# One kernel's first 75 microseconds: loads first, tables on ScalarE's queue, two low halves on VectorE, bias transfers later

## The reference

```python
hn = rms_norm(h, attn_norm[0])
qkv = hn @ w_qkv + b_qkv                       # 1024 q, 128 k, 128 v columns
q = q_columns * HEAD_DIM ** -0.5
s = einsum('bqhgd,bshd->bhgqs', q, k) + head_bias(rel_table, dist)
s = where(in_window & valid, s, NEG_INF)       # window of 128 keys
p = softmax(s, with a sink per head); o = p @ v
h = h + o @ w_o + b_o
h = h + swiglu(rms_norm(h, ffn_norm[0]), w_gu, w_down)
```

## Time and profile before

| | |
|---|---|
| three runs, us | 1986.18, 1988.04, 1989.64 |
| median, us | 1988.04 |
| profiled execution, us | 1987.46, of which the span 1985.7 |
| busy share of the span | PE 97%, PEld 81%, DVE 53%, ACT 42%, POOL 40% |
| chain that ended last | PE 66%, issue 19%, POOL 8%, DVE 5%, ACT 2% |
| weight loads | 294 of 512 KB, median 3.5 us to landing |

### The profile page before, as it was taken

The page is one execution under the profiler, slowest core; times in us unless marked ns, Lnnn a source line. Parts: engine busy times, 40 slices in busy tenths (PEclk is TensorE's granted clock), DMA queues, the critical chain, the costliest instruction groups (busy, mean ns, idle before and its releaser), DMA issues.

```text
span 1985.7 us, 29356 instructions
## 1 busy us (share of the span) xinstructions
PE 1925.1 (97%) x9732; PEld 1617.1 (81%) x9732; DVE 1047.3 (53%) x2320; ACT 831.9 (42%) x1528; POOL 800.7 (40%) x395
## 2 busy tenths in 40 slices
PE   7999999999999999999999999999999899999997
PEld 5898888888878899888888887888788788777886
DVE  5565656221354777545562445656514656565645
ACT  4564222222353777542222323322222346666622
POOL 3633544444364111135444443444544233323441
PEclk9999999999999999999999999999999999999999
DMA  7632554332233113025543322223222121212121
GB/s 238 183 101 96 201 177 162 106 104 95 85 127 121 39 52 89 33 96 201 176 163 105 106 95 90 91 96 111 96 95 95 64 85 54 74 50 77 64 86 43
DMA packets 70019, 209.50 MB, mean 106 GB/s; under 512 B 9739, under 2 KB 15115, under 8 KB 69948
## 3 DMA queue, kind: packets, MB, share of 16 engines
q1 hardware_dynamic: 57724, 174.72, 26.8%
q10 hardware_dynamic: 12224, 33.85, 5.3%
HBM read 196.90 MB, written 8.49 MB: 103 GB/s over the span
## 4 chain that ended last, share of the span: by engine, by line
PE 66%; issue 19%; POOL 8%; DVE 5%; ACT 2%; POOLq 0%; DVEq 0%; ACTq 0%
PE bank L1019 16%; PE bank L1021 15%; PE bank L1020 15%; POOL wsp L470 8%; PE bank L1372 3%; PE bank L1321 2%; PE bank L1567 2%; PE bank L1422 2%; PE bank L1352 2%; PE bank L1223 1%; PE bank L1548 1%; PE bank L1559 1%; PE bank L1427 1%; PE bank L1368 1%; PE bank L1211 1%
## 5 line engine op out<-in xcount | busy, mean ns | idle before, releaser
L470 POOL TENSOR_TENSOR wsp<-raw,wsp 128x1024 fp32r<-128x1024 f32 (+2 forms) x294 | 713.4, 2433 | 942.5 <-ACT wsp L574 942.2
L1019 PE MATMUL bank<-xs,wsp 128*128 128x512 f32 x1304 | 513.8, 394 | 5.0 <-POOL wsp L470 2.4
L574 ACT ACTIVATE wsp<-raw 128x1024 fp32r<-128x1024 f32 (+2 forms) x294 | 302.6, 1037 | 512.5 <-PE bank L1021 469.0
L1021 PE MATMUL bank<-xs,wsp 128*128 128x512 f32 x1304 | 508.8, 390 | 0.0
L1020 PE MATMUL bank<-xs,wsp 128*128 128x512 f32 x1304 | 508.4, 390 | 0.0
L1019 PEld LDWEIGHTS bank<-xs,wsp 128*128 128x128 f32 x1304 | 245.6, 188 | 58.1 <-issue 8.4
L1021 PEld LDWEIGHTS bank<-xs,wsp 128*128 128x128 f32 x1304 | 245.3, 188 | 51.9
L1020 PEld LDWEIGHTS bank<-xs,wsp 128*128 128x128 f32 x1304 | 245.7, 188 | 50.1 <-issue 1.0
L1019 PE MATMUL bank<-gsp,wsp 128*128 128x512 f32 x512 | 200.1, 391 | 2.1 <-issue 1.2
L1021 PE MATMUL bank<-gsp,wsp 128*128 128x512 f32 x512 | 199.3, 389 | 0.0
L1020 PE MATMUL bank<-gsp,wsp 128*128 128x512 f32 x512 | 199.2, 389 | 0.0
(11 more groups left out here) (319 smaller groups left out, 2746.5 us busy)
## 6 DMA issues: line engine op xcount, KB each, us to landing
raw<-weights SPq DMA_DIRECT2D x294, 512.0 KB, 3.5
gen<-ada ACTq DMA_DIRECT2D x48, 512.0 KB, 3.6
tmp<-mid SPq DMA_DIRECT2D x64, 128.0 KB, 3.0
bias_b<-bias_row ACTq DMA_DIRECT2D x1, 4096.0 KB, 37.9
mid<-bias_b SPq DMA_DIRECT2D x8, 512.0 KB, 4.0
hT<-xT SPq DMA_DIRECT2D x2, 1024.0 KB, 9.5
bias_a<-bias_row ACTq DMA_DIRECT2D x1, 2048.0 KB, 17.7
mid<-bias_a SPq DMA_DIRECT2D x8, 256.0 KB, 3.0
```

The costliest lines, as they stand in the source:

```text
L470: pool.tensor_tensor(wsp[:, slot, 1, 0:w], raw[:, slot, 0:w], wsp[:, slot, 0, 0:w].bitcast(F32), ALU.subtract).then_inc(w_ready, 1)
L574: act.activation(wsp[:, u % RING, 0, 0:w], raw[:, u % RING, 0:w], ACT.Copy).then_inc(hi_done, 1)
L1019: pe.matmul(dst, w[0], x[0], start=first, stop=False)
L1021: return pe.matmul(dst, w[1], x[0], start=False, stop=last)
```

## The change

The order of the first 75 us is rewritten. Nothing behind the query units changes.

- SyncE begins with unit 0. `rel` and `onehot` move to ScalarE's queue, ahead of `colp` and `rowp`, behind the wait for the first memset.
- ScalarE runs a tiny Copy (one column) before it waits for data; the instruction stream places a table load ahead of the first activation.
- VectorE makes the low halves of units 0 and 1: unit 0 before the input's low halves, unit 1 behind them. GpSimd begins with unit 2, once `w_ready` is 2.
- ScalarE's order becomes: split unit 0, scale 4 tiles, split unit 1, scale 4 tiles, split unit 2, squares, split unit 3, copy and store the bias product, root, split unit 4, copy k, split units 5 and 6, issue `bias_a` and `bias_b`, split units 7 to 12.
- The bias product goes to banks 3 to 6 instead of 1 to 4. TensorE waits for its copies before the first query unit, not before `A_V`.
- TensorE runs filling matmuls of 128 x 128 into bank 7, which nobody reads: 9 at the start, and 2 behind each of the four bias matmuls.

```diff
 @block.sync
-            sp.wait_ge(consts, 1)
-            sp.dma_start(gen[0:32, 0:HEADS], rel).then_inc(rel_in, 16)
-            sp.dma_start(gen[0:33, 16:16 + BIAS_COLS], onehot).then_inc(rel_in, 16)
 @block.gpsimd
-            split_units(0, A_O + AHEAD)
+            pool.wait_ge(w_ready, 2)
+            for u in range(2, RING):
+                split_lo(u, u)
+            split_units(RING, A_O + AHEAD)
 @block.scalar
+            act.wait_ge(consts, 1)
+            act.dma_start(gen[0:32, 0:HEADS], rel).then_inc(rel_in, 16)
+            act.dma_start(gen[0:33, 16:16 + BIAS_COLS], onehot).then_inc(rel_in, 16)
             act.dma_start(colp[:, :], cols).then_inc(cols_in, 16)
             act.dma_start(rowp[:, :], rows.partition_broadcast(P)).then_inc(rows_in, 16)
+            act.wait_ge(consts, 4)
+            act.activation(credit[:, 11:12], eps[:, 0:1], ACT.Copy)
...
+            def bias_rows():
+                act.wait_ge(brow_mm, 4)
+                for n in range(4):
+                    w = BIAS_COLS // 4
+                    act.activation(brow[:, w * n:w * n + w], bank[3 + n][0:HEADS, 0:w], ACT.Copy).then_inc(brow_copied, 1)
+                act.wait_ge(brow_copied, 4)
+                act.dma_start(bias_row, brow).then_inc(bias_stored, 16)
             split_hi(0)
-            scaled_hi("attn0", 0)
-            for u in range(1, AHEAD):
-                split_hi(u)
...
+            scaled_hi("attn0", 0, range(4))
+            split_hi(1)
+            scaled_hi("attn0", 0, range(4, DC))
+            split_hi(2)
+            squares(0, (A_K + AHEAD,), bias_rows)
             split_hi(A_V + AHEAD)
             act.wait_ge(k_raw, 1)
             act.activation(a_ks[0:HD], a_k, ACT.Copy).then_inc(k_hi, 1)
-            with act.Fori(0, 2) as i:
-                for k in range(RING):
-                    split_hi(A_Q + k + AHEAD, i)
+            for u in range(A_Q + AHEAD, A_Q + DC + AHEAD):
+                split_hi(u)
+                if u == A_Q + AHEAD + 1:
+                    act.wait_ge(bias_stored, 16)
+                    act.dma_start(bias_a, ...).then_inc(bias_stored, 16)
+                    act.dma_start(bias_b, ...).then_inc(bias_stored, 16)
 @block.tensor
+            def keep_running(dst, count):
+                for _ in range(count):
+                    pe.matmul(dst[:, 0:P], mean_w[:, :], ident[:, :], start=True, stop=True)
+            pe.wait_ge(consts, 6)
+            keep_running(bank[7], 9)
             pe.wait_ge(rel_in, 32)
             for n in range(4):
                 w = BIAS_COLS // 4
-                pe.matmul(bank[1 + n][0:HEADS, 0:w], ...)
+                pe.matmul(bank[3 + n][0:HEADS, 0:w], ...)
+                keep_running(bank[7], 2)
-            pe.wait_ge(consts, 6)
             project(A_K, bank[0][:, :], norm=0)
-            pe.wait_ge(brow_copied, 4)
             project(A_V, bank[1][:, :])
             mean_square(0)
             for i in range(2):
                 if i:
                     ...
+                else:
+                    pe.wait_ge(brow_copied, 4)
 @block.vector
+            def split_lo(u):
+                dve.wait_ge(hi_done, u + 1)
+                if u:
+                    dve.wait_ge(w_ready, u)
+                dve.tensor_tensor(wsp[:, u % RING, 1, :], raw[:, u % RING, :], wsp[:, u % RING, 0, :].bitcast(F32),
+                                  ALU.subtract).then_inc(w_ready, 1)
+            split_lo(0)
             dve.wait_ge(cols_in, 16)
             scaled_lo(0, "attn0")
+            split_lo(1)
```

More of the change, by code:

```diff
@@ L574, in split_hi, with scaled_hi @@
                 act.activation(wsp[:, u % RING, 0, 0:w], raw[:, u % RING, 0:w], ACT.Copy).then_inc(hi_done, 1)
-            def scaled_hi(gain, base):
-                for j in range(DC):
+            def scaled_hi(gain, base, tiles=range(DC)):
+                for j in tiles:
                     if base:
@@ L583, in scaled_hi, with squares @@
                     act.activation(xs[:, 0, j, :], hT[:, j, :], ACT.Copy, scale=col(gain, j)).then_inc(xs_hi, 1)
-            def squares(n, held=()):
+            def squares(n, held=(), between=None):
                 if n >= NORM_FINAL:
@@ L600, in squares @@
                     split_hi(u)
+                if between is not None:
+                    between()
                 act.wait_ge(sq_used, 8 * n + 8)
@@ L663, in ffn @@
                 out_inputs(u0 + 2 * FC, FC, MID_FFN[n], n == 1)
+            act.wait_ge(consts, 1)
+            act.dma_start(gen[0:32, 0:HEADS], rel).then_inc(rel_in, 16)
+            act.dma_start(gen[0:33, 16:16 + BIAS_COLS], onehot).then_inc(rel_in, 16)
             act.dma_start(colp[:, :], cols).then_inc(cols_in, 16)
             act.dma_start(rowp[:, :], rows.partition_broadcast(P)).then_inc(rows_in, 16)
+            act.wait_ge(consts, 4)
+            act.activation(credit[:, 11:12], eps[:, 0:1], ACT.Copy)
             act.wait_ge(cols_in, 16)
             act.wait_ge(consts, 6)
-            split_hi(0)
-            scaled_hi("attn0", 0)
-            for u in range(1, AHEAD):
-                split_hi(u)
[L675 to L688, removed]
+            def bias_rows():
[5 more added lines that the diff above has]
+                act.dma_start(bias_row, brow).then_inc(bias_stored, 16)
+            brow = gen[0:HEADS, 2048:2048 + BIAS_COLS]
+            split_hi(0)
+            scaled_hi("attn0", 0, range(4))
[3 more added lines that the diff above has]
+            squares(0, (A_K + AHEAD,), bias_rows)
             split_hi(A_V + AHEAD)
@@ L691, in _ @@
             act.activation(a_ks[0:HD], a_k, ACT.Copy).then_inc(k_hi, 1)
-            with act.Fori(0, 2) as i:
-                for k in range(RING):
-                    split_hi(A_Q + k + AHEAD, i)
+            for u in range(A_Q + AHEAD, A_Q + DC + AHEAD):
+                split_hi(u)
+                if u == A_Q + AHEAD + 1:
+                    act.wait_ge(bias_stored, 16)
+                    act.dma_start(bias_a, bass.AP(bias_row.tensor, 127, [[BIAS_COLS, HEADS], [-1, P], [1, 256]])
+                                  ).then_inc(bias_stored, 16)
+                    act.dma_start(bias_b, bass.AP(bias_row.tensor, 384 + 127, [[BIAS_COLS, HEADS], [-1, P], [1, 512]])
+                                  ).then_inc(bias_stored, 16)
             def queries_hi(b, e, loaded):
@@ L1171, in _ @@
                 w = BIAS_COLS // 4
-                pe.matmul(bank[1 + n][0:HEADS, 0:w], gen[0:33, 0:HEADS], gen[0:33, 16 + w * n:16 + w * n + w],
+                pe.matmul(bank[3 + n][0:HEADS, 0:w], gen[0:33, 0:HEADS], gen[0:33, 16 + w * n:16 + w * n + w],
                           start=True, stop=True).then_inc(brow_mm, 1)
-            pe.wait_ge(consts, 6)
+                keep_running(bank[7], 2)
             project(A_K, bank[0][:, :], norm=0)
-            pe.wait_ge(brow_copied, 4)
             project(A_V, bank[1][:, :])
```

## The result

| | before | after |
|---|---|---|
| median of 22 runs, us | 1989.40 | 1995.22 |
| lowest to highest, us | 1985.45 to 1997.40 | 1989.54 to 2001.79 |
| profiled execution, us (span) | 1987.46 (1985.7) | 2000.39 (1998.7) |

The ratio is 1.0023, with a 95% interval of 1.0013 to 1.0032: slower by 4.6 us (2.6 to 6.4). Forecast were 1993.5 us, in 1985.5 to 1997.5. The two medians are 5.8 us apart, within the same interval.

The account below looks back on a forecast made before the run. Two chains were taken to end together at attention's start: TensorE's query units and SyncE's wait for bias_b. 1987.46 + 4.3 (later release) + 1.3 (clock) = 1993.1, as a median 1993.5 us; range 1985.5 to 1997.5.

Parts of the forecast that it names:

- Release of SyncE: SyncE's wait for bias_b before the first query loads: ends at 72.2 instead of 67.87, making attention's scores 4.3 us later.
- D: Time from the first bias transfer's issue to SyncE's release: 38.6 us before, taken as 35.9 after, bounds 31 to 38.6.
- rival 1: Bias is there in time: D under 33 us, release before 69.5, 1.5 us gained, 1986.5 in all; chance 0.20.
- Held adds: VectorE's adds before the sum of squares: GpSimd's splits hold two, so they end at 28.1, about as before (28.03).
- Rival 2: Nothing holds VectorE's adds: they end at 25.8, and with a short D TensorE is 3.8 us early, 1984.2; chance 0.10.
- TensorE's own chain: TensorE up to attention: unit 3's 1.54 us wait goes, so the last query unit ends at 73.5 instead of 75.0.
- the worth 0 of the fillers: TensorE's 17 filling matmuls at the start: worth between -0.9 and +0.1 us at the sum of squares, taken as 0.
- the cold case: TensorE stays at 1.2 GHz through the first units: A_V ends at about 29, against 23.7 if warm.
- First loads: Unit 0 and the input's halves land some 0.95 us earlier: halves at 9.4 and 13.4 instead of 10.36 and 14.35.
- Clock: After 6.6 us idle before attention, TensorE starts at half clock: +1.3 us, between 0 and 2.6.
- rival 3: Adds held once, D as taken: issue at 34.0, release at 69.9, +2.0 us, no clock loss, 1990; chance 0.15.
- rival 4: The low clock lasts through attention's first pair: 2.6 us more than taken, issue at 37.9, 1998; chance 0.05.

Follow-up runs that it names:

- the last experiment: Changed kernel without fillers, colp first on ScalarE's queue, GpSimd behind the adds, bias_b on its own count, sinks copied first; 0.9974 of the kernel before.
- the first experiment: Changed kernel with the two bias transfers issued behind the root again, as in the kernel before; 1.0004 of the kernel before.
- the old order with an own count: Kernel before with bias_b counted on another semaphore, so the first query loads need bias_a only; 1.0003 of the kernel before.

## Why the prediction was right, and where it was off

**Release of SyncE: right.** Said were issue 36.3, D 35.9, release 72.2, scores 80.1; measured 37.92, 35.0, 72.91, 80.58 (+4.8 for +4.3). Part of this closeness is luck. The k rows were done at 37.7 instead of 35.1, 2.6 us late, for the sum of squares came late (see TensorE's chain below). The issue followed them by 0.2 us, where the prediction had taken 1.2 for ScalarE's work between: ScalarE issued the transfers without waiting for the copy of k and the two splits to be through. That leaves the issue 1.6 us late, and D was 0.9 shorter, which takes most of it back again. D fell from 38.6, but not simply with the loads beside it: over the kernels it was 36.3 for an issue at 32.33, 33.1 for 33.10, 35.5 for 37.09, 33.7 for 37.22. What else sets it stays open; rival 1 needed under 33, and no kernel in which SyncE waits for it had that. That the transfer had no slack holds: from SyncE's release to the query splits it is 4.31 to 4.34 us in the four kernels in which they wait for the loads, and 4.51 in the kernel before, so it had 0.2 us of slack. Undoing that one edit, or taking SyncE's wait away, removes the loss from the medians; making it alone brings one.

**Held adds: right.** Two of over 2 us, where the blocks were put. The Trainium skill's rule (SBUF — State Buffer, "Who interferes with whom") holds in these traces: 2.89 us for an add of 0.69 in the changed kernel, and none held in the experiment in which GpSimd starts behind them. Rival 2's condition, nothing holds the adds, had to be made by an edit; then its 3.8 us are there on TensorE's chain (3.5), but not at the scores, since D did not become short enough.

**TensorE's own chain: wrong by 2.4 us.** Its end had no effect, since TensorE waited for the queries anyway; its start, the late sum of squares, went into the issue of the transfers. The prediction had the last query unit end at 73.5. It ends at 75.91, and in the kernel before at 75.05. The 1.54 us of unit 3's wait were gained as foretold, but the sum of squares came at 30.83 instead of 28.1, and two steps failed there. The first is the adds: they ended at 29.54, 1.4 us late, since the input was scaled late (next paragraph). The second is the worth 0 of the fillers: `A_V` ended another 1.3 us later. The bias matmuls began at 8.04, not 6.5, since `onehot` now lands later, and the last filler ended at 18.6, not 16.8. And the 29 for the cold case was a wrong sum: from 16.8 on, 48 matmuls at 0.23 us, 13 of them 0.19 slower as in the earlier trace rows, end at about 30.3, 2.2 us behind the adds' 28.1. By the prediction's own numbers the fillers cost time on TensorE's chain unless they warmed it.

**First loads: wrong.** The halves of the input were to come at 9.4 and 13.4. The first was scaled from 11.73, because `colp` held the split of unit 0, and scaling, until 10.77. The prediction has no term for `colp`, though its place behind `rel` and `onehot` stands in the change. The DMA issues of the first 20 us show its landing, before first, then after:

```profile
colp<-cols ACTq DMA_DIRECT2D x1, 79.5 KB, 2.0
```

```profile
colp<-cols ACTq DMA_DIRECT2D x1, 79.5 KB, 8.7
```

It is issued at 2.04 instead of 0.82, behind `onehot` and beside weights and input, and lands 8.7 us later instead of 2.0. But the 0.95 us would have been missed without it too: in the last experiment, where `colp` is early and scaling waits for the input alone, the halves are scaled from 10.70 and 14.71, against 10.36 and 14.35 before. With the input issued 1 us earlier and the tables on the other queue it came no sooner. So late `colp` cost 0.2 to 1.0 us on the first half (it is scaled from 10.93 without the fillers), and the earlier issue was worth nothing.

**Clock: right in kind.** Granted 0.50 behind a pause. Taken were 1.3 us for it; the lag behind the kernel before grows by 1.0 us in the first 7 us of attention, until the clock is up. Another 0.5 come before 117 us at a clock of 1.00 and are not its price. The pause was 4.7 us, not 6.6, for TensorE came later by itself. What the prediction did not have is that a clock loss of this size or more stands behind attention's start without such a pause too: 2.3 us in the first experiment's trace and 2.9 in that of the old order with an own count, after waits of 0.8 and 1.5 to 1.9 us.

**The sum** of +5.6 to the profiled execution stands beside +4.6 (2.6 to 6.4) by the ratio, +5.8 by the medians and +6.3 at 117 us in the trace. Rival 1 fell with D, rival 3 by the second held add. The low clock did not last through the pair (1.00 from 88), against rival 4.

## What to carry to other kernels

When a transfer is issued later, ask who waits for its count, and whether that waiter needs it: here one shared count let a 4 MB transfer for the second layer hold back the first layer's queries. When an engine gets a head start, look at which other engine the same event releases: VectorE's low half of unit 1 released GpSimd, whose split held VectorE's very next add for 2 us, and the head start was gone. When a small transfer that everything waits for moves back in its queue, find out what covers its landing; here it cost up to 1.0 us, and moving it to the front won nothing, since the input was the next thing to wait for. And follow a gain past the place where it is made: the traced execution of the first experiment started attention 3.5 us earlier than the changed kernel and was only 0.9 ahead of it at 84 us.

## What the runs showed of the hardware

- A VectorE copy of 2 columns took 1.24 us instead of 0.16 when a GpSimd split had begun 0.13 us ahead of it.
- Nine 128-column float32 matmuls without a break (4.21 us), then narrow ones mixed with more fillers until 18.6, did not leave TensorE at its full pace: 0.43 us a matmul until 21.4, though the granted column says 1.00 from 16 to 24. In the first experiment's trace, with the same fillers, it says 0.50 from 12 to 20. The granted column of the first 20 us can't be relied on in these traces; the pace of equal matmuls can.
- ScalarE issued a transfer 0.2 us after it had begun a copy of 1.06 us, and 0.8 us before the two splits that stand ahead of the transfer in its program (37.74, 37.92, 38.70). It is the same with the transfers late in the old order (36.91, 37.09, 37.88). So in these traces the transfers were late by the wait for k that they stood behind, not by the work in front of them.
- A wait of 3.0 us in the kernel without fillers left TensorE at 0.43 us a matmul for the next eight; one of about 1.1 us at the same place in the kernel before did not.
- The same two waits before the scores (0.8 and 0.6 us) left the clock at 1.00 in one kernel and at 0.72 in another. What decides between them stays open.
